# RG-LRU gate products of a hybrid decoder step as four 64 by 64 tiles in two PSUM banks

## The reference

```python
xh = xc.reshape(Bn, T, A_HEADS, A_HEAD_DIM)        # 8 heads of 64 channels
r = jax.nn.sigmoid(jnp.einsum('bthi,hij->bthj', xh, w_ra) + b_ra).reshape(Bn, T, W_A)
ig = jax.nn.sigmoid(jnp.einsum('bthi,hij->bthj', xh, w_rx) + b_rx).reshape(Bn, T, W_A)
log_a = -RG_C * r * jax.nn.softplus(-lam)
a = jnp.exp(log_a)
bt = jnp.sqrt(-jnp.expm1(2.0 * log_a)) * ig * xc
_, hs = lax.associative_scan(_lin_combine, (a, bt), axis=1)
```

## Time and profile before

| what | value |
|---|---|
| median of 3 runs | 2454.43 us (2454.26 to 2455.49) |
| the profiled execution's own time | 2457.05 us |
| its span, first to last instruction | 2455.2 us |
| PE matmuls busy | 2393.2 us (97%) |
| DVE busy | 940.7 us (38%) |
| ACT busy | 643.8 us (26%) |
| POOL busy | 287.6 us (12%) |
| granted TensorE clock, mean | 0.989 of full speed |
| share of PE in the chain that ended last | 88% |

### The profile page before, as it was taken

The page is one execution under the profiler, slowest core; times in us unless marked ns, Lnnn a source line. Parts: engine busy times, 40 slices in busy tenths (PEclk is TensorE's granted clock), DMA queues, the critical chain, the costliest instruction groups (busy, mean ns, idle before and its releaser), DMA issues.

```text
span 2455.2 us, 38591 instructions
## 1 busy us (share of the span) xinstructions
PE 2393.2 (97%) x15842; PEld 2148.2 (87%) x15842; DVE 940.7 (38%) x1593; ACT 643.8 (26%) x1199; POOL 287.6 (12%) x276
## 2 busy tenths in 40 slices
PE   7999998999999999999999999999999999999997
PEld 5777786888888888888898899999999999999996
DVE  6766564421121121223765566544212211211224
ACT  5345343331131121223334234422201201200211
POOL 0000002222122122222000000010000100000000
PEclk9999998999999999999999999999999999999998
DMA  5332325444444434454422222332222232223223
GB/s 199 108 114 97 109 91 176 137 156 143 151 133 149 153 130 153 144 201 145 138 96 69 70 70 87 98 136 91 90 86 86 88 100 86 85 85 93 95 86 106
DMA packets 88162, 284.39 MB, mean 116 GB/s; under 512 B 15856, under 2 KB 19056, under 8 KB 88048
## 3 DMA queue, kind: packets, MB, share of 16 engines
q1 hardware_dynamic: 46512, 158.09, 19.0%
q0 software_dynamic: 27648, 100.68, 12.7%
q10 hardware_dynamic: 13888, 23.95, 2.9%
HBM read 171.07 MB, written 111.62 MB: 115 GB/s over the span
## 4 chain that ended last, share of the span: by engine, by line
PE 88%; DVE 6%; issue 3%; ACT 2%; ACTq 1%; DMA 0%; POOL 0%; DVEq 0%; POOLq 0%
PE bank L476 28%; PE bank L478 27%; PE bank L477 27%; PE aux L617 1%; PE aux L543 1%; DVE a_lo L1178 1%; DVE xc L1361 1%; PE aux L571 1%; ACT s_in L726 1%; PE aux L594 1%; PE aux L593 1%; PE aux L548 0%; DVE xy L1287 0%; DVE rs L1122 0%; DVE xy L1113 0%
## 5 line engine op out<-in xcount | busy, mean ns | idle before, releaser
L476 PE MATMUL bank<-a_hi,w_hi 128*128 128x358 f32 (+3 forms) x2560 | 923.8, 361 | 31.1 <-DVE a_lo L1178 11.4
L477 PE MATMUL bank<-a_lo,w_hi 128*128 128x358 f32 (+3 forms) x2560 | 906.7, 354 | 0.0
L478 PE MATMUL bank<-a_hi,w_lo 128*128 128x358 f32 (+3 forms) x2560 | 906.6, 354 | 0.0
L476 PEld LDWEIGHTS bank<-a_hi,w_hi 128*128 128x128 f32 x2560 | 485.8, 190 | 82.6 <-POOL w_lo L431 19.3
L478 PEld LDWEIGHTS bank<-a_hi,w_lo 128*128 128x128 f32 x2560 | 486.5, 190 | 43.6
L477 PEld LDWEIGHTS bank<-a_lo,w_hi 128*128 128x128 f32 x2560 | 486.4, 190 | 42.9 <-issue 1.5
L476 PE MATMUL bank<-b_hi,w_hi 128*128 128x358 f32 (+3 forms) x1280 | 450.2, 352 | 0.0
L477 PE MATMUL bank<-b_lo,w_hi 128*128 128x358 f32 (+3 forms) x1280 | 449.1, 351 | 0.0
L478 PE MATMUL bank<-b_hi,w_lo 128*128 128x358 f32 (+3 forms) x1280 | 449.1, 351 | 0.0
L1489 DVE TENSOR_TENSOR xy<-xy,bank 128x356 f32 (+6 forms) x160 | 94.1, 588 | 554.9 <-PE bank L478 554.9
L726 ACT ACTIVATE a_hi<-tmp 128x356 f32 (+5 forms) x160 | 88.3, 552 | 817.3 <-DVE tmp L1479 817.3
(11 more groups left out here) (162 smaller groups left out, 1417.3 us busy)
## 6 DMA issues: line engine op xcount, KB each, us to landing
w_st<-in_wall SPq DMA_DIRECT2D x96, 512.0 KB, 4.1
kept_hi<-w_hi SPq DMA_DIRECT2D x96, 512.0 KB, 4.9
kept_lo<-w_lo SPq DMA_DIRECT2D x96, 512.0 KB, 5.7
w_hi<-kept_hi POOLq DMA_DIRECT2D x96, 512.0 KB, 4.0
w_lo<-kept_lo POOLq DMA_DIRECT2D x96, 512.0 KB, 4.7
xs<-in_xT ACTq DMA_DIRECT2D x8, 536.0 KB, 7.5
xy<-in_xT ACTq DMA_DIRECT2D x8, 536.0 KB, 8.3
xy<-in_xT ACTq DMA_DIRECT2D x8, 512.0 KB, 7.7
```

What stands on the lines that cost most here:

```text
L476: pe.matmul(ps, wh, xh, start=(j == 0), stop=False)
L477: pe.matmul(ps, wh, xl, start=False, stop=False)
L478: mm = pe.matmul(ps, wl, xh, start=False, stop=(j == 7))
```

## The change

The block diagonal matrices `w_ra` and `w_rx` give way to one tensor `w_gate`. It holds the four 64 by 64 blocks of a head pair: those of the first gate on the diagonal, those of the second off it. Each gate of a token tile is now two matmuls with 64 rows and 64 columns. The second gate's two halves come out with their partitions exchanged, so that the four matmuls use the four quarters of the array and two banks. ACT reads the first gate's bank whole, as before, and the second gate's bank in two activations of 64 partitions, each writing to the other half of `ig`, with a bias vector `b_rx_turned` whose halves are exchanged. One release of the bank stands at the second of the two. SP loads w_gate in four DMAs and b_rx_turned in two, where there were two DMAs.

```diff
-        w_ra = sb("w_ra", [P, 4, P])
-        w_rx = sb("w_rx", [P, 4, P])
+        w_gate = sb("w_gate", [P, 4, P])
+        b_rx_turned = sb("b_rx_turned", [P, 4])
+        def gate_half(h):
+
+            return slice(64 * h, 64 * h + 64)
...
-            sync.dma_start(w_ra[:, :, :], wra_d).then_inc(const_in, 16)
-            sync.dma_start(w_rx[:, :, :], wrx_d).then_inc(const_in, 16)
+            for h in range(2):
+                r_, o_ = gate_half(h), gate_half(1 - h)
+                sync.dma_start(w_gate[r_, :, r_], wra_d[r_, :, r_]).then_inc(const_in, 16)
+                sync.dma_start(w_gate[r_, :, o_], wrx_d[r_, :, r_]).then_inc(const_in, 16)
+                sync.dma_start(b_rx_turned[o_, :], par_d[r_, PC["b_rx"]:PC["b_rx"] + 4]).then_inc(const_in, 16)
...
                     pe.wait_ge(rg_step, rg_at(p, i, "sc3" if p else "c3"))
                     for t, (c0, w) in enumerate(TILES[p]):
-                        for g, wt in enumerate((w_ra, w_rx)):
+                        for g in range(2):
                             ps = open_bank(a + 2 * t + g)
-                            pe.matmul(ps[:, 0:w], wt[:, i, :], xc[:, c0:c0 + w], start=True,
-                                      stop=True).then_inc(aux_done, 1)
+                            for h in range(2):
+                                r_, o_ = gate_half(h), gate_half(h ^ g)
+                                mm = pe.matmul(ps[o_, 0:w], w_gate[r_, i, o_], xc[r_, c0:c0 + w], start=True,
+                                               stop=True)
+                            mm.then_inc(aux_done, 1)
...
                     for t, (c0, w) in enumerate(TILES[p]):
-                        for g, (dst, b) in enumerate(((ta, "b_ra"), (ig, "b_rx"))):
-                            u = a + 2 * t + g
-                            filled(act, u)
-                            fn(dst[:, c0:c0 + w], aux[u % 4][:, 0:w], ACT.Sigmoid,
-                               bias=col(b, i)).then_inc(aux_free[u % 4], 1)
+                        u = a + 2 * t
+                        filled(act, u)
+                        fn(ta[:, c0:c0 + w], aux[u % 4][:, 0:w], ACT.Sigmoid,
+                           bias=col("b_ra", i)).then_inc(aux_free[u % 4], 1)
+                        u += 1
+                        filled(act, u)
+                        for h in range(2):
+                            r_, o_ = gate_half(h), gate_half(1 - h)
+                            ins = fn(ig[r_, c0:c0 + w], aux[u % 4][o_, 0:w], ACT.Sigmoid, bias=b_rx_turned[o_, i:i + 1])
+                        ins.then_inc(aux_free[u % 4], 1)
```

More of the change, by code:

```diff
@@ L512, in piece @@
                     if n == 0:
-                        pe.wait_ge(const_in, 16 * 3)
+                        pe.wait_ge(const_in, 16 * 7)
                     for t in range(NT[p]):
@@ L902, in piece @@
                 elif name == "GATE":
+                    if n == 0:
+                        act.wait_ge(const_in, 16 * 7)
                     if i > 0:
```

## The result

The changed kernel is slower: 2464.88 us median (2464.38 to 2466.23, 6 runs) against 2454.55 for the kernel before on the same chip, a ratio of 1.0040 with a 95% interval of 1.0030 to 1.0049. That is 10.3 us more, where no change was forecast, and it lies 0.9 above the range. The profiled execution took 2464.87 us, its span is 2463.0, its mean granted clock 0.987 (0.989 before).

A forecast was written before the change was run, and what follows sets the result against it. PE was 88% of the chain that ended last. Pass 0's +0.8 and pass 1's -1.0 us summed to -0.2 on the profiled 2457.05, so 2456.8; the median, 2.6 below, gave 2454.2 us, range 2451.0 to 2464.0.

The forecast's parts named there:

- What the gates cost PE: PE time of the gates before the change, four heads: 13.7 us in pass 0 and 14.4 in pass 1, 28.1 together.
- side by side: PE's four array quarters run at once: a token tile's two gates take 0.86 us for 1.72, or 0.60 for 1.20.
- shape change: On PE, changing tile shape costs 0.09 us into and 0.19 out of each GATE, 0.28 in all.
- B: On PE, two row tiles can't write one PSUM bank at a time: 9.2 us more, 2463.7; chance 0.13.
- C: On PE a matmul's two records stay in order, only the next one's first overlaps: 5.9 us more, 2460.3; chance 0.10.
- D: No overlap at all between row tiles on PE: 30.8 us more, 2485; chance 0.06.
- ACT, the new pace: GATE sigmoids run back to back, 0.61 us apart in pass 0 and 0.48 in pass 1; low end 0.48, 0.38.
- Pass 0, who decides: In pass 0 DVE's u follows Tanh 0.2 us later, L1's wait eats PE's saving: +0.8 us, four heads (-1.2 to +1.0).
- Rival A: In pass 0 L1's wait isn't tied to the GATE, 1.43 us a head kept: 6.7 less, 2447.7; chance 0.06.
- The clock: Sign of a wholly wrong forecast: the granted clock, full through pass 0's heads, falls in the longer waits; no size given.
- Pass 1: In pass 1 PE's GATE waits for a bank but saves 0.26 us a head: -1.0 us, four heads (-1.8 to -0.4).
- The rest: SP's four more DMAs of constants end at 9.8 us, before the next load at 10.90: no cost.

The follow-up runs named there:

- The halves alone: Kernel before, TensorE unchanged, with the second gate read by ACT in two activations of 64 partitions, not exchanged: 2458.99 us, ratio 1.0011.
- Whole activations: Changed kernel with the second gate's bank read whole in one sigmoid, its halves left exchanged: 2446.99 us, ratio 0.9971.
- Filling them: Changed kernel with 12 extra products of ones on PE ahead of L1's wait in pass 0: 2459.79 us, ratio 1.0017.
- the move of GB: DVE's scan chain of the previous head moved from slot 0 to 8 of pass 0: 2457.65 us in the changed kernel, 2463.07 in the one before.
- the move of GATE: Heads 1 to 3's GATE in pass 0 moved from slot 16 to 14: changed kernel 2462.93 us, kernel before 2450.95; changed with GA at slot 16, 2461.96.

## Why the prediction was wrong

- **What the gates cost PE, side by side, shape change: right.** 1.87 us for a GATE of pass 0, and entry and exit together 0.08 over the forecast. Rivals B, C and D fall: the four first records of a group start within 0.02 us in the kernel with only pass 1 changed, two of them in each bank. B's time (2463.7) is close to the measured one by accident: its mechanism isn't there. The Trainium skill (TensorEngine Tiling (Array Packing), Restrictions and Gotchas, Gotcha 1) holds that different row tiles can't access one PSUM bank at once. The rows of the kernel with only pass 1 changed show two row tiles writing different partitions of one bank within 0.52 us, so here the measurement decides against it.
- **ACT, the new pace: mis-sized.** I took 0.61 for a step, from whole activations in a row, and wrote that half the partitions save nothing. What they do is cost: every step is 0.70. Five steps make 0.45 of the difference, which puts u 0.65 late in place of 0.2. Four heads: +2.6 us in place of +0.8. The halves alone measured +2.9. The bound that I gave, 0.48 to 0.61, didn't hold the value, since it reached only to rows of one kind. For the low spacing I wrote Tanh's end as 157.2 and L1 0.3 earlier; the same sum gives 157.1 and 0.4.
- **Pass 0, who decides: right.** L1 follows u at 14.35 us in both kernels, and the saving of PE is eaten by the wait. Rival A was excluded for the right reason. Whole activations come near its time (2446.99 against 2447.7), but from another sum: L1 still waits for u, and the gain is 1.16 a head in pass 0 (1.43 in A) and 0.74 in pass 1 (0.26).
- **The clock: the step that failed.** The sum took every wait at its length. I named a falling clock as what would make the whole wrong, but gave it neither a price nor a chance. The waits came out at 2.7 to 3.0 us (2.2 forecast), and behind each the clock was 0.50 for 3.4 us. Filling them gave 5.6 us back. The price could have been read beforehand: I looked at the clock in pass 0's heads alone, and the same trace has it at half behind waits of 1.96 and 2.27 us in pass 1. So the forecast wait of 2.2 was already one behind which the clock might fall; L1 waits of 2.2 weren't tried, and the shortest L1 waits with falls were 2.4.
- **Pass 1: the mechanism right, the gain not.** The wait for the third token tile's bank is there. It shows as 0.3 idle where 1.2 was forecast, since the first gate's pair of the third tile runs in it from 1337.35 on. The release came 2.65 behind the GATE's start (2.50 forecast) with steps of 0.57 for 0.48, so 0.05 a head are saved in place of 0.26. That pass alone measured 1.0002 with an interval of 2 us each way, which holds both.
- **The rest: the price right, the sizes not.** I forecast the last constant to be issued by 9.8 us, under cover of the next load's wait until 10.90. SP's issues of the six took 0.61 to 2.50 us each and ended at 14.22, and the next load started at 14.60. The one behind it started at 16.50 against 17.00, and head 0's GATE at 73.31, within the 72.3 to 73.9 of all kernels here. So no cost shows.

The ledger against the kernel before: 4 x 0.65 for u, 4 x 1.5 for the clock, -0.2 for pass 1, 8.4 us. The two profiled executions differ by 7.8 and the medians by 10.3, since the profiled one of before was 2.6 above its median. By place, the changed kernel's profile loses 1.1 up to the first L1 of pass 0 and 6.7 from there to the fourth. Behind that both take 2131.2, though the fourth fall lies there: the profile of before has 7 us more at half clock elsewhere in that part (37.5 against 30.7, the last stretch of each left out). So falls that no edit touches move the total by a few us, and the ledger is good to that.

## What to carry to other kernels

When a saving on the bounding engine turns into a wait of that engine, price the clock behind the wait too, from every stretch at half clock in the trace and not only from the part that the edit touches. Here a stop that grew from 0.6 to 2.8 us cost 1.5 more in the products after it, more than twice the 0.65 of the later release itself. A matmul layout that makes its reader work in halves should be costed on the reader first, each step at the full length of an activation. When the freed time can't be used, the release must come earlier (a shorter chain on ACT and DVE), and any move of pieces has to be followed on every engine: the move of GB only traded L1's wait for one at U, and the move of GATE made L1's wait longer.

## What the runs showed of the hardware

- Two 64-row tiles that write different partitions of one PSUM bank run fully side by side, fp32 with two records each: 16 records of 512 columns in 1.87 us.
- In these rows activations from PSUM overlap their neighbour only when the operands read and those written begin on the same partitions in both. Start to start at 512 columns: whole to whole 0.58, whole to lower half 0.59, lower to upper half 0.69, upper half to whole 0.71; with shifted halves in the order of the change every step 0.70; four halves in pairs of the same partitions took 2.53, two pairs of different ones 2.76.
- A granted clock of 0.50 stood behind L1 waits of 2.4 to 3.6 us, mostly for 3.4 us, for 6.8 behind two of the four in the changed kernel with the GATE earlier. It came behind three of four waits of 2.4 to 2.5 in each of two executions, behind none of four up to 2.83 in another, and behind all four of up to 3.40. In pass 1 of the kernel before it came behind waits of 1.96 and 2.27 and not behind 1.84, but behind 1.83 in pass 1 of the changed kernel with GB later (1315.7 and 1493.2, 6.8 us each). So the length of the wait alone doesn't decide it. Behind waits of up to 1.15 it didn't come in pass 0's heads. Times of kernels with waits near 2.4 spread by 11 us between executions, where the kernel before spreads by 5 on the same chip.
- Each fall of 3.4 us costs 1.5 us: (80.62 - 78.54) less 0.58 of added work, and 5.6 / 4 = 1.4 by filling the waits.
